# VectorE's remainder of a pair behind the next block's remainders, and another order of the work around a feed-forward's norm

## What is computed

```python
def rmsnorm(x, g):
    xf = x.astype(jnp.float32)
    inv = lax.rsqrt(jnp.mean(xf * xf, axis=-1, keepdims=True) + EPS)
    return (xf * inv).astype(x.dtype) * g

def swiglu(h, wg, wu, wd):
    return (jax.nn.silu(h @ wg) * (h @ wu)) @ wd

for i in range(DEPTH):
    xp = xp + 0.5 * swiglu(rmsnorm(xp, norm_ffn1[i]), w_ffn1_gate[i], w_ffn1_up[i], w_ffn1_down[i])
    ...                                      # the mixer
    xp = xp + 0.5 * swiglu(rmsnorm(xp, norm_ffn2[i]), w_ffn2_gate[i], w_ffn2_up[i], w_ffn2_down[i])
```

## Time and profile before

| | us |
|---|---|
| median of 3 runs | 2475.04 |
| the runs | 2477.73, 2470.79, 2475.04 |
| the profiled execution, whole | 2488.74 |
| its span, first to last instruction | 2486.9 |
| TensorE busy with matmuls | 2338.0 (94%) |
| VectorE busy | 1676.6 (67%) |
| ScalarE busy | 1172.1 (47%) |
| GpSimd busy | 480.2 (19%) |
| mean granted TensorE clock, share of full | 0.980 |

### The profile page before, as it was taken

One profiled execution on the slowest core, in us unless ns is written; L12 is line 12 of the kernel. 1 busy time (PEld: TensorE's weight loads), 2 busy tenths in 40 slices (PEclk: granted clock), 3 DMA queues, 4 the chain that ended last, 5 costly groups with the idle time before them and its releaser, 6 DMA issues.

```text
span 2486.9 us, 47320 instructions
## 1 busy us (share of the span) xinstructions
PE 2338.0 (94%) x17889; PEld 2250.6 (91%) x17889; DVE 1676.6 (67%) x2599; ACT 1172.1 (47%) x2162; POOL 480.2 (19%) x342
## 2 busy tenths in 40 slices
PE   7899999999999999999799999899999999899998
PEld 7899899875999999999799999889999999799998
DVE  7778775546555555547877777877776666877774
ACT  4445454464455555534445454445453224454542
POOL 0243430000000000000244330234340000244340
PEclk9899999979999999999999999899999999899999
DMA  4778764310211111203678764678763333577772
GB/s 129 169 190 202 182 165 122 88 44 25 60 30 49 49 45 43 61 18 94 161 196 199 185 166 113 152 180 200 186 175 102 94 90 98 131 184 195 186 201 81
DMA packets 502368, 313.30 MB, mean 126 GB/s; under 512 B 36352, under 2 KB 484950, under 8 KB 502152
## 3 DMA queue, kind: packets, MB, share of 16 engines
q1 hardware_dynamic: 486420, 253.67, 35.8%
q0 software_dynamic: 15552, 56.63, 13.1%
q10 hardware_dynamic: 180, 0.11, 0.0%
HBM read 250.89 MB, written 2.87 MB: 102 GB/s over the span
## 4 chain that ended last, share of the span: by engine, by line
PE 57%; DMA 15%; DVE 12%; issue 6%; ACT 5%; POOL 4%; SPq 1%; ACTq 0%; DVEq 0%; POOLq 0%
PE ps L2030 15%; PE ps L552 6%; PE ps L556 6%; PE ps L554 6%; PE ps L951 5%; PE ps L953 5%; PE ps L952 5%; DMA wsum75b<-raw 5%; DMA raw<-in_w_ffn_up 5%; DMA raw<-in_w_ffn_down 3%; POOL wsum L737 2%; POOL wsum L735 1%; DVE w_lo L653 1%; DVE w_lo L683 1%; DMA wsum<-raw 1%
## 5 line engine op out<-in xcount | busy, mean ns | idle before, releaser
L951 PE MATMUL ps<-hs,w_hi 128*128 128x260 f32 x1440 | 416.4, 289 | 43.1 <-DVE w_lo L653 17.8
L952 PE MATMUL ps<-hs,w_hi 128*128 128x260 f32 x1440 | 411.8, 286 | 0.0
L953 PE MATMUL ps<-hs,w_lo 128*128 128x260 f32 x1440 | 411.4, 286 | 0.0
L951 PEld LDWEIGHTS ps<-hs,w_hi 128*128 128x128 f32 x1440 | 276.0, 192 | 51.7 <-DVE w_lo L653 21.7
L952 PEld LDWEIGHTS ps<-hs,w_hi 128*128 128x128 f32 x1440 | 276.8, 192 | 0.0
L953 PEld LDWEIGHTS ps<-hs,w_lo 128*128 128x128 f32 x1440 | 275.9, 192 | 0.0
L2077 ACT ACTIVATE ksq<-ps 128x384 f32<-128x384 f32 (+1 forms) x384 | 146.7, 455 | 196.6 <-PE ps L2030 196.6
L951 PE MATMUL ps<-hs,x_hi 128*128 128x260 f32 x688 | 200.8, 292 | 27.8 <-DVE x_lo L653 15.3
L737 POOL TENSOR_TENSOR wsum<-wsum,raw 128x512 f32<-128x512 f32 x108 | 210.9, 1953 | 8.5
L952 PE MATMUL ps<-hs,x_hi 128*128 128x260 f32 x688 | 197.9, 288 | 0.0
L953 PE MATMUL ps<-hs,x_lo 128*128 128x260 f32 x688 | 197.7, 287 | 0.0
(11 more groups left out here) (409 smaller groups left out, 6341.5 us busy)
## 6 DMA issues: line engine op xcount, KB each, us to landing
raw<-in_w_ffn_gate SPq DMA_DIRECT2D x88, 512.0 KB, 4.0
raw<-in_w_ffn_up SPq DMA_DIRECT2D x88, 512.0 KB, 5.2
raw<-in_w_ffn_down SPq DMA_DIRECT2D x64, 512.0 KB, 5.5
wsum<-raw POOLq DMA_DIRECT2D x56, 512.0 KB, 5.6
wsum75b<-raw POOLq DMA_DIRECT2D x52, 512.0 KB, 5.8
cache<-in_cache_latent SPq DMA_DIRECT2D x128, 128.0 KB, 2.0
raw<-in_w_ffn_down SPq DMA_DIRECT2D x32, 384.0 KB, 3.5
raw<-in_w_conv_in SPq DMA_DIRECT2D x24, 512.0 KB, 3.8
```

Of the source, the lines that this page charges most:

```text
L951: nc.tensor.matmul(o, hi[:, kc], mh[:, xc], start=start and k == 0, stop=False, skip_group_check=goes_on)
L952: nc.tensor.matmul(o, hi[:, kc], ml[:, xc], start=False, stop=False, skip_group_check=goes_on)
L953: mm = nc.tensor.matmul(o, lo[:, kc], mh[:, xc], start=False, stop=k == KH - 1, skip_group_check=goes_on)
```

## The change

There are two edits of order and no new instruction.

1. In blocks after block 3, `pair_lo` is no longer between `first_begun` and `first_lo`, but the last step of the block, behind `m63_lo` of the next block. Block 3 stays as it was.
2. Between the norm and block 3, VectorE's steps for the second half of the sets are ordered anew: the hidden tile of block 1 comes ahead of set 2, `first_lo` of block 3 and the remainder of set 2 come between set 2 and set 3, the scaling of block 2's gate comes after set 3. ScalarE rounds set 3 ahead of the silu of block 2.

```diff
@@ ffn_act
             set_hi(act, at, 2)
+            set_hi(act, at, 3)
             silu(own[2])
-            set_hi(act, at, 3)
             m63_hi(act, own[3])
@@ ffn_dve, block
                     first_begun(bk)
-                    if done:
-                        last_lo(dve, done) if done.last else pair_lo(dve, done)
+                    if done and done.last:
+                        last_lo(dve, done)
                     plain_lo(dve, nxt) if nxt.plain else first_lo(dve, nxt)
                 first_made(bk)
                 up_made(bk)
                 if bk.out:
                     first_out(bk)
                 if not nxt.plain:
                     m63_lo(dve, nxt)
+                if early and done and not done.last:
+                    pair_lo(dve, done)
@@ ffn_dve, after the norm
             up_lo(dve, own[2])
+            plain_hid(own[1])
             scaled_dve(dve, at, 2)
             set_mix(dve, at, 2)
-            plain_hid(own[1])
-            scale_gate(own[2])
+            first_lo(dve, own[3])
+            set_lo(dve, at, 2)
             scaled_dve(dve, at, 3)
             set_mix(dve, at, 3)
-            first_lo(dve, own[3])
-            set_lo(dve, at, 2)
+            scale_gate(own[2])
             set_lo(dve, at, 3)
             m63_lo(dve, own[3])
```

## The result

| | us |
|---|---|
| before, median of 4 runs | 2476.39 |
| after, median of 4 runs | 2510.03 (2507.31 to 2515.15) |
| ratio, 95% interval | 1.0119 (1.0089 to 1.0149) |
| the profiled execution of after, whole | 2507.31 |
| its span | 2505.4 |

The change makes the kernel 1.2% slower: 33.6 us by the medians, 29.5 by the ratio (22 to 37). The two profiled executions lie only 18.5 us apart. So a term read from this pair of traces shows where time goes, and its size is weighed by the timed experiments.

A forecast was written before the change was run, and what follows sets the result against it. TensorE, busy 94% of the span, was taken as the bound, so order only changes its waits: 8.4 + 37.6 + 15.2 - 11.8 - 20 = +29.4 us on 2475.0 gives 2504.4 us, range 2483 to 2529.

The forecast's parts named there:

- D heads: Heads of D9 and D21: TensorE waits for pair_lo behind m63_lo, 4.7 us longer at each of eight, +37.6 us.
- S heads: S blocks behind a pair-making block: 23.5 us of waits for first_lo go, half is kept, -11.8 us.
- what is late next there: S blocks: later m75_lo returns 0.7 of 1.05 us as a wait at the fifth half product.
- the loop I named: S blocks: m4_lo, raw row load, GpSimd's DMA and sums, m63_hi, m63_lo; closes every two blocks, as long as TensorE's two.
- The clock: Behind the late heads of D9 and D21: granted clock falls, 1.9 us lost at each of eight, +15.2 us.
- Absorbed at third half products: D9 to S14 and D21 to S28: two thirds of 28.5 us of waits taken back, -20 us (ends 8 and 28).
- The rival in which the loop carries all: D9 and D21: late m4_lo, some 5.2 us each, passed on every two blocks, nothing absorbed; +50 us, 2525; chance 0.22.
- Edit 2: Norm ahead of S3: last set_lo ends 2.1 us later in four feed-forwards, +8.4 us (bounds 5 and 10).
- The rival of cancelling parts: S blocks keep all 23.5 us and 28 are absorbed, so edit 1 comes to +1.3 us; total 2485; chance 0.2.
- The prediction's strict reading: D9 and D21 heads: GpSimd contention gives back all 2.05 us of pair_lo at each, making the sum 8.4 us smaller.

The follow-up runs named there:

- e1: Edit 1 alone, with the norm's order as before, against the kernel before: +19.3 us, ratio 1.0078.
- e3: Edit 1 only where the next block is an S block, norm as before, against the kernel before: -5.0 us, ratio 0.9980.
- e9: Kernel before with pair_lo of S4, S6, S14, S16, S18 moved between up_made and m63_lo of the next block: -17.1 us, ratio 0.9931.
- e7: Kernel before with pair_lo of S4, S6, S14, S16, S18 moved between m75_lo and m4_lo of the next block: -18.6 us; repeated, -16.9.
- e8: Kernel before with pair_lo of S8 and S20 alone moved between up_made and m63_lo: +4.0 us, ratio 1.0016.
- e4: Edit 1 only where the next block is D9 or D21, norm as before, against the kernel before: +21.5 us, ratio 1.0087.
- e2: Edit 2 alone, with pair_lo where it stood before, against the kernel before: +8.9 us, ratio 1.0036.
- e5: Edit 2 alone, with set 2's remainder put back behind set 3's making and the scaled gate, against the kernel before: +2.7 us, ratio 1.0011.
- e6: Kernel before with pair_lo of S4, S6, S14, S16, S18 moved behind m4_lo in the next block: -13.4 us, ratio 0.9946.

## Why the prediction came out, step by step

The sign, the place and the total were right: 2504.4 forecast, 2510.03 measured. The total is better than its parts. Edit 1 was to cost 21.0 us and cost 19.3 (e1), made of two terms that were both too high and of opposite sign: 32.8 for the D heads, measured 21.5, and -11.8 for the S heads, measured -5.0. That these errors nearly cancel is luck.

- **S heads, forecast -11.8.** The waits for L653 went, as said. Too large a part was kept: e3 measures -5.0, though its interval reaches -10.4. The step that failed is "what is late next there". I had the return at the fifth half product, for L683; that was 3.6 us in the changed kernel. The larger ones are 11.6 us at the third and 4.3 at the seventh (0.3 before), and in e3 the low clock in five blocks, a term I had put at nothing here. I took `pair_lo` as 2.05 us added ahead of `m75_lo`, and didn't ask whether VectorE waits ahead of `m63_lo`. Once `first_lo` is early it waits there up to 3.64 us, and `pair_lo` was queued behind. e9 gains 12 us by this place alone, and e7 shows that the loop I named, through `m4_lo` and the raw row, is not what binds.
- **D heads, forecast 37.6.** The chain was right in each link. The waits for L815 come to 38.4 us, where 8.7 stood before, so 29.7 in place of 37.6: 3.7 us a head, where I took 4.7 (lower bound 3.2). One reason is GpSimd: its two sums take 3.1 us on average at the eight heads, 4.8 before, so it gives back 1.7 us and not the 1.0 I took.
- **The clock, forecast 15.2.** 16.2 us over undisturbed blocks, 14.0 over what D9 and D21 took without waits before. It was read from one stretch and held in sum, with 1.5 to 2.8 us a head. The premise, that only a wait longer than the usual ones brings it on, is wrong: e8 has it after 2.1 to 3.1 us. No experiment isolates it from the wait.
- **Absorbed at third half products, forecast -20.** Between D9 and S14 and between D21 and S29 these waits fell from 29.0 us to 4.0: 25 us. What I held against it, that D9's own late `m75_lo` and `m4_lo` are passed on, doesn't show: D10 to D12 run at 10.1 us each. The rival in which the loop carries all, at 2525, is out. These three parts as measured, 29.7 + 14.0 - 25 = 18.7, are near the 21.5 of e4; as forecast they made 32.8. That is no close check: by length from head to head, D9 and D21 are 36.9 us longer than before in this pair of traces and the blocks behind them, to S14 and S28, 26.5 shorter, which makes 10.4, and the profiled execution of before lay 12.3 us above its median.
- **Edit 2, forecast 8.4.** 8.9 by e2; the idle times were forecast as 0.75 and 1.3 and are 0.65 and 1.16; e5 gives it back by giving back the cover.
- **The rival of cancelling parts, 2485,** needed 23.5 us kept in the S blocks. e3 says no for this order of the steps; e7 and e9 say that nearly all of it is there for another order.

So the best kernel here is e7 (or e9, which can't be told from it): about 17 us faster than the kernel before.

## What to carry to other kernels

When a step that nobody waits for is moved back to free the one behind it, put it where its engine would stand idle, not behind the next wait: a step queued behind a wait adds its length after the wait, and what follows is late by both. Never move it across its own consumer's need: the same step was spare ahead of S blocks and the last thing wanted ahead of D9 and D21, and one condition in the code separates -5.0 us (e3) from +19.3 (e1). And where two engines hand pieces to each other (ScalarE rounds, VectorE takes the remainder), a reordering that leaves a piece without enough other work beside its rounding costs what is left uncovered, here 0.65 and 1.16 of 1.71 us, though the sum of work is unchanged.

## What the runs showed of the hardware

GpSimd's sums of 128x512 take longer beside VectorE's work. In the trace of before there are 164 of them (L735 and L737). The 17 that ran beside no VectorE instruction with two operands in SBUF took 1.27 to 1.29 us, the other 147 took 1.90 on average and up to 3.14. VectorE pays too: `first_lo` took 1.21 to 1.23 us when no such sum ran beside it and up to 2.36 when one did. The same 108 instructions of L737, in the changed kernel:

```profile
L737 POOL TENSOR_TENSOR wsum<-wsum,raw 128x512 f32<-128x512 f32 x108 | 184.6, 1709 | 8.5
```

Before they took 210.9 us, 1953 ns each. In all GpSimd's busy time fell by 42 us with no instruction less. At the eight D heads the pair of sums fell by 1.7 us on average when `pair_lo` (2.05 us) no longer ran beside them. The Trainium skill ("GPSIMD Engine Reference", section 1, Specifications) has GpSimd and VectorE in contention for SBUF under VectorE instructions with two inputs there; the trace agrees, with the 1.28 and 1.90 us above. The prediction's strict reading of it would have given back all 2.05 us, and 1.7 is nearer to that than to the 1.0 of my sum. No run changes the overlap and nothing else.

The clock fell after shorter waits than I had thought: in e8 the eight D heads waited 2.07 to 3.08 us, and six of the blocks D9 and D21 behind them took 11.5 to 11.7 us without waits inside, the other two 10.1 and 10.4. For D21 the granted clock was 0.71 over 5.9 us, as shown. In e7 the heads waited 1.39 to 1.99 us, and all eight blocks took 10.2. The waits of 3.8 to 6.3 us in the changed kernel were followed by 11.6 to 12.9 us for the same blocks. So a wait of 4 to 6 us cost 1.5 to 2.8 us of the clock, and one of 2 to 3 us, where it cost anything, 1.4 to 1.6.

The length of the wait alone doesn't tell which it will be. In e6 a head of D9 waited 1.91 us and the block behind it, all 84 matmuls, had a granted clock of 0.85:

```profile
1260.50:1272.10 11.60, 11.60 (x84) 11.60 (x85) 8.24 (x13) 5.43 (x8) 3.16 (x4) 0.85 0.82 187
```

In e9 a head of D21 waited longer, 2.27 us, and its 84 matmuls ran at full clock:

```profile
270.40:280.40 10.00, 10.00 (x84) 10.00 (x85) 7.52 (x13) 5.33 (x8) 2.60 (x2) 1.00 0.97 213
```
